# Returning expert results to their tokens: one DRAM row per token and choice in place of selection products

## The reference, cut to what matters

```
logits = h @ router                       # 256 x 8
top_vals, top_idx = top_k(logits, 2)      # two experts for each token
gates = softmax(top_vals)
gate_e = sum(one_hot(top_idx) * gates)    # 256 x 8, zero where not chosen
for e in range(8):
    out = out + gate_e[:, e] * ((silu(h @ wg[e]) * (h @ wu[e])) @ wd[e])   # 1024 -> 3584 -> 1024
x = x + out;  x = rmsnorm(x, final_norm)
```

## Time and profile before

| | us |
|---|---|
| three runs | 2585.18, 2580.52, 2580.43 |
| median | 2580.52 |
| span of the profiled execution | 2584.9 |
| PE busy | 2500.7 (97%) |
| DVE busy | 1807.1 (70%) |
| ACT busy | 1447.6 (56%) |
| POOL busy | 71.3 (3%) |
| DRAM read, written | 633.07 MB, 7.86 MB |

### The profile page before, as it was taken

How to read it: one execution, slowest core, us unless ns; L and a number is a source line. 1 busy time by engine, 2 the same in 40 slices (tenths; PEclk the granted TensorE clock), 3 DMA queues, 4 the chain that set the end, 5 groups by cost and what they waited for, 6 DMA issues and landing times.

```text
span 2584.9 us, 32744 instructions
## 1 busy us (share of the span) xinstructions
PE 2500.7 (97%) x11767; PEld 1991.6 (77%) x11767; DVE 1807.1 (70%) x1708; ACT 1447.6 (56%) x1564; POOL 71.3 (3%) x54
## 2 busy tenths in 40 slices
PE   7999999989999999999999998999999999998999
PEld 6678887667788888888888786888884687777887
DVE  6564446557999999989998986645544575777544
ACT  4554434546777777777777775435443343466443
POOL 0000000011000000000000000600000000000000
PEclk9999999889999999999999999999999999999999
DMA  6885542659999999999999996655543344434652
GB/s 219 313 312 180 192 165 98 245 179 360 393 371 365 367 371 365 363 368 361 365 357 388 341 346 221 227 186 188 184 162 118 119 131 135 131 98 162 228 191 69
DMA packets 330911, 642.13 MB, mean 248 GB/s; under 512 B 14441, under 2 KB 113289, under 8 KB 330633
## 3 DMA queue, kind: packets, MB, share of 16 engines
q1 hardware_dynamic: 328088, 631.02, 69.8%
q0 software_dynamic: 2736, 9.96, 1.0%
HBM read 633.07 MB, written 7.86 MB: 248 GB/s over the span
## 4 chain that ended last, share of the span: by engine, by line
PE 87%; DVE 6%; ACT 4%; DMA 2%; issue 1%; SPq 0%; POOL 0%; DVEq 0%; ACTq 0%; POOLq 0%
PE ps L950 21%; PE ps L863 19%; PE ps L990 11%; PE ps L905 10%; PE ps L1370 6%; PE ps L795 5%; PE ps L1399 2%; PE ps L1301 2%; PE ps L1104 1%; PE ps L838 1%; DVE As L2403 1%; PE ps L876 1%; PE ps L975 1%; DVE Bs L2493 1%; DVE ringL L2373 1%
## 5 line engine op out<-in xcount | busy, mean ns | idle before, releaser
L2403 DVE TENSOR_TENSOR As<-ringA,As 128x2048 fp32r<-128x2048 f32 x316 | 727.0, 2301 | 188.0 <-ACT As L1690 115.6
L950 PE MATMUL ps<-As,xgs 128*128 128x512 f32 x2688 | 646.3, 392 | 7.7 <-DVE As L2403 6.2
L950 PEld LDWEIGHTS ps<-As,xgs 128*128 128x128 f32 x2688 | 498.9, 188 | 114.7 <-issue 5.3
L1779 ACT ACTIVATE As<-ringA 128x2048 fp32r<-128x2048 f32 x224 | 428.8, 1914 | 107.4 <-PE ps L950 101.9
L863 PE MATMUL ps<-As,xs 128*128 128x512 f32 x1408 | 361.3, 394 | 0.0
L990 PE MATMUL ps<-Bs,hds 128*128 128x512 f32 x1320 | 319.4, 391 | 4.1 <-DVE hds L2474 2.5
L863 PEld LDWEIGHTS ps<-As,xs 128*128 128x128 f32 x1408 | 261.9, 188 | 55.9
L990 PEld LDWEIGHTS ps<-Bs,hds 128*128 128x128 f32 x1320 | 246.4, 188 | 60.2 <-issue 7.3
L2493 DVE TENSOR_TENSOR Bs<-ringB,Bs 128x2048 fp32r<-128x2048 f32 x110 | 251.8, 2289 | 19.6 <-ACT Bs L1818 18.6
L905 PE MATMUL ps<-Bs,hds 128*128 128x512 f32 x1056 | 247.9, 390 | 0.0
L1818 ACT ACTIVATE Bs<-ringB 128x2048 fp32r<-128x2048 f32 x110 | 211.2, 1920 | 63.4 <-PE ps L990 62.1
(11 more groups left out here) (424 smaller groups left out, 3228.5 us busy)
## 6 DMA issues: line engine op xcount, KB each, us to landing
ringA<-in_moe_w_gate SPq DMA_DIRECT2D x112, 1024.0 KB, 6.9
ringA<-in_moe_w_up SPq DMA_DIRECT2D x112, 1024.0 KB, 6.7
ringB<-in_moe_w_down SPq DMA_DIRECT2D x112, 1024.0 KB, 6.9
ringA<-in_w_ff_in SPq DMA_DIRECT2D x132, 512.0 KB, 4.7
ringA<-in_w_in SPq DMA_DIRECT2D x56, 1024.0 KB, 5.3
ringA<-in_w_ada SPq DMA_DIRECT2D x36, 1024.0 KB, 6.5
ringB<-in_w_ff_out SPq DMA_DIRECT2D x33, 1024.0 KB, 5.0
ringA<-in_dense_w_gate SPq DMA_DIRECT2D x28, 512.0 KB, 3.6
```

What stands on the lines that cost most here:

```text
L950: m = mm(ps[:, bank, :], lhs(l, tt, k), As[:, h, r, k % 4, :], start=k == 0 and n == 0, stop=k == KC - 1 and n == 2)
L1779: A(As[:, h, 0, :, :], ringA[:, (p["a"] + u) % 2, 4 * h:4 * h + 4, :], ACT.Copy).then_inc(A_high, 1)
L2403: V.tensor_tensor(As[:, h, 1, :, :], ringA[:, (p["a"] + u) % 2, 4 * h:4 * h + 4, :], f32(As[:, h, 0, :, :]), ALU.subtract).then_inc(A_spli ...
```

## The change

- The results of an expert are no longer brought back by products. `one_hot` (gated), the transposes of `selg`, `gate_sums`, `y_low`, `scatter`, `add` and the idle products go.
- A DRAM tensor `results` has a row per token and choice (512), and rows beyond for slots without a token. It is cleared by POOL with four more DMAs behind the nine of `taken`.
- A DRAM tensor `owner` holds for each expert and slot the number of the result row and the gate. POOL fills it first with rows beyond, then, behind the four writes into `taken`, writes it with four indirect DMAs of eight bytes per token and choice, waits for them, and loads it into `slot_of`. `places()` works out `mine` (row number and gate) before it lets POOL go on (`placed` 6 instead of 4).
- ACT's `keep_y` copies the expert's gate column (1 column), waits for that copy and for the expert before's write to have landed, writes `ye` unrounded in fp32 and itself frees the accumulator. POOL then writes `ye` to `results` with one indirect DMA per expert.
- After the eighth write has landed, POOL loads the two halves of `results`, each 1 MB, into `hT` and the arena; DVE adds both to x (128x2048 each) behind the first block of `ff0c`. The final norm and the transposes that follow it come one block later than before in each stream, and `head` is 3 instead of 2.
- If the second path is taken, `mine` points beyond the 512 rows, and what DVE adds is the cleared zeros.

```diff
+SKIP = 2 * SEQ
+NROWS = 2 * SKIP + P
...
+    parts["row"] = np.arange(P)[:, None] + P * np.arange(2 * TILES)[None, :]
...
+        results = nc.dram_tensor("results", (NROWS, D), F32, kind="Internal").ap()
+        owner = nc.dram_tensor("owner", ((NE + 1) * P, 2), U32, kind="Internal").ap()
+        mine = sb("mine", [P, 2 * TILES, 2], U32)
+        slot_of = sb("slot_of", [P, NE + 1, 2], U32)
...
-        ye = arenaR[:, 1024:1024 + D], hTR[:, 0:4, :].rearrange("p k n -> p (k n)")
+        ye = ar(1024, D)
+        returned = hT[:, :, :].rearrange("p k n -> p (k n)"), ar(0, TILES * D)
...
             def turn_taken(e):
                 pe.wait_ge(rows_back, 16 * e)
-                if not isinstance(e, int) or e >= 2:
-                    pe.wait_ge(added, 2 * e - 2)
+                pe.wait_ge(xg_ready, 2 * e)
...
-            def scatter(e, tt):
...
-                    for q in range(2):
-                        last = mm(ps[:, bank + half, :], selT[:, tt, :], ye[q][:, half * 512:(half + 1) * 512], start=q == 0, stop=q == 1)
-                last.then_inc(mixed_back, 1)
...
                 def after(n):
-                    if n in (2, 3) and not first:
-                        scatter(e - 1, n - 2)
-                    if n == NB1 - 2:
-                        pe.wait_ge(selg_ready, e + 1)
-                        for tt in range(TILES):
-                            last = tr(ps[:, 3, tt * P:(tt + 1) * P], selg[:, tt, :], ident)
-                        last.then_inc(selg_tp, 1)
-                        if not final:
-                            turn_taken(e + 1)
+                    if n == NB1 - 2 and not final:
+                        turn_taken(e + 1)
...
                 expert(NE - 1)
-                idle_products(2)
-                for tt in range(TILES):
-                    scatter(NE - 1, tt)
...
# GpSimd
+            for g in range(2 * TILES):
+                pool.dma_start(results[g * P:(g + 1) * P, :].rearrange("p (a b) -> p a b", a=4), blank.unsqueeze(1).broadcast_to([P, 4, 256])).then_inc(cleared, 16)
...
+            pool.dma_start(owner.rearrange("(e s) c -> s e c", s=P), slot_of[:, :, :]).then_inc(unnamed, 16)
...
-            pool.wait_ge(placed, 4)
+            pool.wait_ge(placed, 6)
             for j in range(2 * TILES):
                 pool.indirect_dma_start(out=taken[:, :], ...).then_inc(put, 16)
+            pool.wait_ge(unnamed, 16)
+            for j in range(2 * TILES):
+                pool.indirect_dma_start(out=owner[:, :], out_offset=bass.IndirectOffsetOnAxis(ap=place[:, j:j + 1], axis=0), in_=mine[:, j, :], in_offset=None).then_inc(named, 16)
+            pool.wait_ge(named, 16 * 2 * TILES)
+            pool.dma_start(slot_of[:, :, :], owner.rearrange("(e s) c -> s e c", s=P)).then_inc(scattered, 16)
+            pool.wait_ge(scattered, 16)
+            for e in range(NE):
+                pool.wait_ge(acc_free, ph["moe"]["f"] + e + 1)
+                pool.indirect_dma_start(out=results[:, :], out_offset=bass.IndirectOffsetOnAxis(ap=slot_of[:, e, 0:1], axis=0), in_=ye, in_offset=None).then_inc(scattered, 16)
+            pool.wait_ge(scattered, 16 * (NE + 1))
+            for choice in range(2):
+                pool.dma_start(returned[choice].rearrange("p (t n) -> p t n", t=TILES), results[choice * SEQ:(choice + 1) * SEQ, :].rearrange("(t p) n -> p t n", p=P)).then_inc(results_in[choice], 16)
...
# ScalarE
             def keep_y(e):
+                act.wait_ge(scattered, 16 * e + 16)
+                A(small[:, 354:355], slot_of[:, bass.ds(e, 1), 1].bitcast(F32), ACT.Copy).then_inc(gcol_kept, 1)
+                act.wait_ge(gcol_kept, e + 1)
                 act.wait_ge(down_done, e * (2 * NB1) + (ph["moe"]["s"] + 2 * NB1))
-                act.wait_ge(selgT_ready, e + 1)
-                A(ye[0], ps[:, 4:6, :].rearrange("p a b -> p (a b)"), ACT.Copy, scale=small[:, 354:355]).then_inc(y_high, 1)
+                A(ye, ps[:, 4:6, :].rearrange("p a b -> p (a b)"), ACT.Copy, scale=small[:, 354:355]).then_inc(acc_free, 1)
...
# VectorE
             def places():
...
                 V.tensor_copy(place[:, :], to).then_inc(placed, 1)
+                V.tensor_copy(mine[:, :, 1].bitcast(F32), small[:, 310:314])
+                V.tensor_scalar(small[:, 452:453], small[:, 344:345], float(CAP), float(SKIP), ALU.is_gt, ALU.mult).then_inc(placed, 1)
+                dve.wait_ge(placed, 5)
+                V.tensor_scalar(mine[:, :, 0], k1("row"), small[:, 452:453], None, ALU.add).then_inc(placed, 1)
...
             def x_rows(n):
                 if n == 0:
+                    for choice in range(2):
+                        dve.wait_ge(results_in[choice], 16)
+                        last = V.tensor_tensor(flat_x, flat_x, returned[choice], ALU.add)
+                        if choice == 0:
+                            ch.done(last)
+                    last.then_inc(x_ready, 1)
+                if n == 1:
                     dve.wait_ge(nrm_std, SQ["final"])
...
-            feed(ph["ff0c"], 2, ahead=True, head=2, drains=False, after=x_rows, within=x_scale)
+            feed(ph["ff0c"], 2, ahead=True, head=3, drains=False, after=x_rows, within=x_scale)
```

More of the change, by code:

```diff
@@ L1025, in turn_taken @@
                     last.then_inc(gathered, 1)
-            def scatter(e, tt):
-                if tt == 0:
-                    pe.wait_ge(acc_free, e + (moe["f"] + 1))
-                    if not isinstance(e, int) or e < NE - 1:
-                        pe.wait_ge(xg_ready, 2 * e + 4)
-                final = isinstance(e, int) and e == NE - 1
-                if final != bool(tt):
-                    pe.wait_ge(added, 2 * e + tt)
-                bank = 2 if final and tt else 6
-                for half in range(2):
-                    for q in range(2):
-                        last = mm(ps[:, bank + half, :], selT[:, tt, :], ye[q][:, half * 512:(half + 1) * 512], start=q == 0, stop=q == 1)
-                last.then_inc(mixed_back, 1)
             def expert(e):
@@ L2070, in x_rows @@
             def x_rows(n):
-                if n == 1:
+                if n == 2:
                     act.wait_ge(x_ready, XR["moe"])
                     squares(lambda tt: x[:, tt, :], 1, 1e-5, lambda tt, q: x_tok[:, tt, :])
-                if n in (2, 3):
-                    tt = n - 2
+                if n in (3, 4):
+                    tt = n - 3
                     scale, shift = mod_cols(0, 0)
@@ L2101, in context_end @@
                     stats(call["mixc"], [(x_ready, XR["ff0c"])], lambda tt: cs[:, tt, :], eps=1e-6)
-            feed(ph["ff0c"], 2, ahead=True, head=2, drains=False, before=x_rows, within=x_stats)
+            feed(ph["ff0c"], 2, ahead=True, head=3, drains=False, before=x_rows, within=x_stats)
             feed(ph["ff0x"], 2, head=2, leads=False, before=context_end)
@@ L2552, in after @@
                         context_low(n)
-                    if n == 2 and not first:
-                        add(e - 1, 0)
                     if n == 3 and first:
                         places()
-                    if n == 4:
-                        if not first:
-                            dve.wait_ge(selg_tp, e)
-                        one_hot(e, e + 2, True)
                     if n == NB1 - 2 and not final:
@@ L2566, in body @@
                     nxt = (i + 1, 0) if u else (i, 1)
-                    if isinstance(i, int) and i == 1 and u == 0 and not first:
-                        y_low(e - 1)
-                    if last:
-                        gate_sums(e)
                     if not u and not lead:
                         pair_low(e, i - 1)
-                    if isinstance(i, int) and i == 2 and u == 0 and not first:
-                        add(e - 1, 1)
                     if last and final:
@@ L2581, in body @@
                         unit_low(e, *nxt, 0)
-                        y_low(e)
                         unit_low(e, *nxt, 1)
@@ L2879, in _ @@
                 expert(NE - 1)
-                for tt in range(TILES):
-                    add(NE - 1, tt)
-                dve.wait_ge(added, TILES * NE)
             with dve.Else():
```

73 lines of the change are left out of this document (27 added, 46 removed).

## The result

The changed kernel takes 2568.83 us (median of 9 runs, 2563.09 to 2574.25) against 2580.52 (median of 9) for the kernel before. The ratio is 0.9947, 95% interval 0.9933 to 0.996, so 10 to 17 us less. The forecast was 2562.3 us with a range of 2554 to 2576. The profiled execution took 2574.08 us with a span of 2572.3, so it lies 5.3 us above its median, about as the profiled execution of before (2585.2) lies above its own.

The account below looks back on a forecast made before the run. PE was taken to set the pace of the expert loop. The terms, -17.1 - 6.1 + 1.5 + 2.5 + 1.0 = -18.2 us from the 2580.5 us median, gave 2562.3 us, range 2554 to 2576.

Parts of the forecast that it names:

- term 4: Early clearing of result rows: four more clears delay the dense_w_up load near 150 us, +2.5 us, bounds 0 and 5.4.
- Term 1: Expert loop: PE's products, transposes and waits for the hidden block's split go, -17.1 us, at least 12.9.
- Term 2: After the last expert: shorter road to the next feed and less half-speed clock, -6.1 us, bounds 4.6 and 6.4.
- Term 3: Return of the rows after the last write: PE stalls in the feed's second block, +1.5 us, bounds 0 and 9.
- term 5: Places and owners in expert 0: more small DVE operations and small-element transfers, +1.0 us, bounds 0.5 and 3.
- A: Rival: late return of the rows costs 9 instead of 1.5 us, 2569.8 us; chance 0.17.
- B: Rival: early clears and small elements at their upper ends, 5.4 and 3 us, 2567.2 us; chance 0.12.
- C: Rival: DVE becomes the bound in the expert loop and eats the whole 17.1 us, 2579.4 us; chance 0.05.
- D: Rival: the DMA queue bounds the expert loop at 366 GB/s, slower than before, 2589.9 us; chance 0.06.

Follow-up runs that it names:

- c1: Changed kernel plus two idle 128x512 identity products in each of experts 1 to 7, no added DVE work: 2582.4 us, ratio 1.0007 to the kernel before.
- c4: Kernel before without the products of the low part of the expert's result (4 of 8 per expert): 2576.45 us, ratio 0.9982.
- d1: Changed kernel with a2's wait, a later wait for two places, one more weight pair before expert 0's rows, idle products before the last down group: 2553.83 us.
- a1: Changed kernel with only the first fill of the owners moved behind three blocks of the dense feed: 2566.06 us, ratio 0.9926 to the kernel before.
- e3: Changed kernel with the four new clears and the owners' fill moved late, the nine old clears early: 2558.89 us, ratio 0.9912 to the kernel before.
- b1: Kernel before plus only the four clears of the result rows behind the nine old ones: ratio 1.0031, 8.0 us more.
- b2: Kernel before with its nine old clears moved behind the third block of the dense part: ratio 0.9994.
- a2: Changed kernel with all thirteen clears and the owners' fill moved behind three blocks of the dense feed: 2555.49 us, ratio 0.989 to the kernel before.
- c2: Changed kernel with each expert's rows written five times, four of them to tensors nobody reads: 2582.5 us, ratio 1.0001 to the kernel before.
- e2: Changed kernel with only the four new clears moved behind the third dense block, the owners' fill staying early: 2565.8 us, ratio 0.9942 to the kernel before.

## Why the prediction was right, term by term

The range of 2554 to 2576 us holds 2568.8, and the direction and the main mechanism were right: PE's work removed in the loop comes off the end. That the time is as near as 6.5 us to the forecast of 2562.3 is in part luck: term 4 was 7.4 us too low, and the other terms together 7.9 us too high.

| term | predicted | read from the profile after |
|---|---|---|
| 1 loop | -17.1 | -20.7 |
| 2 after the last expert | -6.1 | -7.4 |
| 3 return of the rows | +1.5 | 0 |
| 4 clears, and the fill that was left out of it | +2.5 | +9.9 |
| 5 places and owners in expert 0 | +1.0 | -0.5 |
| sum | -18.2 | -18.7 |

**Term 1** had the right mechanism and was 3.6 us too small. Products and transposes were sized rightly (c1, c4). The time that came with them was about 0.9 us per expert and not 0.35. I had counted only the wait that the list names, and that list counts from the modelled end of the product before, 0.39 us after its start, while products follow each other every 0.23. From start to start the named place has 0.74 us where 0.23 is usual, and 0.33 behind it: 0.6 us. The rest lies in smaller gaps of PE's row of products; which engine made each of them isn't shown. Six periods give 17.8 us, and the last expert, up to its last down group, 2.9.

**Term 2** had 4.6 us for the shorter road and 1.5 for the clock. The road gave 4.15. The reason for the clock was wrong: the half-speed stretch did not go, it moved from the feed to the last down group, where the feed does not feel it: d1 had that group at full speed and its feed began no earlier. What gained 3.25 us by the feed's fifth block was that its first block ran at full speed and that the 1.4 us wait of its third block vanished.

**Term 3** came out at 0, the lower bound. The step that failed is the landing of the last write. I took the 9.8 to 10.9 us of four writes in a row; the last one alone was there within 4.7 us of its issue (1554.84 to 1559.53). That it was alone is not enough, for the seven in the loop were alone too and took 8.9 us in the median, with the engines at share 1.03; from 1554 to 1560 the share was 0.55. The two returns then took 10.3 and 13.0 us, as I had thought. The fit in the Trainium skill, "DMA: Bandwidth & Descriptors", section Anatomy of one DMA, has 3.2 us for the write and 6.8 for the loads: nearer than mine for the first, too low for the second, and right in that the stall is 0.

**Term 4** is the large miss. Its failing step is that the clears "bite only after" 148.5 us and then share the engines half and half, by which only 2.6 of their 5.4 us would reach the weights. In fact the old clears already had the engines to themselves when the load was issued (102.0% from 144 to 146), and with the new ones behind them the weights got 19.2% until 158. So about all of the added bytes came first: 4.9 us (a1 against e3) to 6.3 us (b1), near or over the upper bound. And one part of the change was missing altogether: term 5 counted the 1152 small pieces where the owners are read back, in expert 0, but nobody counted the fill that writes as many of them at 145 us, 3.9 us. Both meet at the place where the chain hangs on one load, and PE had no idle time behind it.

**Term 5** can't be judged by the one pair. Over all profiles without an edit in this stage, expert 0 takes 113.2 us in the mean of the eight with the change and 111.5 in the mean of the four without it, 1.7 us more, where 1.0 was forecast and -0.5 stands in the table. Both groups spread by 2 to 3 us.

**The rest.** The terms sum to -18.7 us, but the medians fell by 11.7, and the ratio gives 10 to 17. For the two profiled executions the gap can be closed. Outside the terms they differ by +4.3 us ahead of the stretch, -2.9 between the dense part and expert 0, and +4.6 behind the feed's fifth block, so with the table's -18.7 it is -12.7, and the span shrank by 12.6. The first of these is chance: it lies before anything of the change has run, and there, from 78 to 88 us, the changed kernel's profile has its clock at 0.50 and the kernel before 1.00. In the thirteen profiles the stretch begins anywhere from 132.9 to 139.6 us, with the change or without. Between whole times, the mean granted clock is part of it: 0.9861 over the changed kernel's runs, against 0.9889 for 23 of the kernel before. 0.0028 of 2570 us is at most 7 us (an estimate, as if PE set the time throughout), or 14 us more at half speed. It goes with the early transfers: the six kernels that have neither the four clears nor the fill early (b2, a2, e3, c4, d1 and the kernel before) have means of 0.9878 to 0.9895, the seven that have one or both 0.9845 to 0.9870. At most 10.2 of the 14 us lie in one half-speed stretch that I can name, behind PE's stall at 163 to 174 us. Why the remainder falls into the same kernels isn't shown; single profiles differ by more than that in where such stretches lie.

**The rivals.** A (late return) did not happen here, but is a real mechanism (c2: 10.95 us of stall). B (the early clears and small elements at their upper ends) did happen at the first place, worse than priced, together with a larger gain. Its 2567.2 us and A's 2569.8 both lie within 2 us of the result, so the time alone would have pointed to a late return that did not happen. C (DVE as the bound) is refuted: PE busy 121.00 of 121, DVE 107.89. D (DMA as the bound of the loop) is refuted: it decided at 370 GB/s, and the loop ran at 380 (45.1 MB in 118.7 us) and, in c2, at 397. The Trainium skill's 358 and 368 GB/s for one core (same page, section Specifications) are not the limit that this kernel meets.

## What to carry to other kernels

Before a transfer is put "early, where it costs nothing", look at how full the DMA engines are there, and by which queue. At share 1.00 the four clears (2.1 MB, 5.2 us at 404 GB/s) delayed the load that the chain waits for by about their full time, and a fill in 8-byte pieces cost many times its bytes (3.9 us at 404 GB/s would be 1.6 MB, and it is 9 KB). Move such preparation to a stretch where the engines have room; here one wait gave back as much as the whole change had brought. When a resource looks like a ceiling (share 1.00, 366 GB/s), ask whether anyone waits for it, since here it was only the demand. And when a forecast comes true, check its terms one by one: this one held while its fourth term was four times too small.

## What the runs showed of the hardware that was not expected

- 1152 pieces of 8 bytes (9 KB) held the 16 DMA engines for some 4 us, at 123 and 187 GB/s and a share of 1.25 and 0.99, where 404 were moved before (102 and 174 GB/s in e2); 128 pieces of 72 bytes did not (337 and 363).
- While the software queue sent its clears, it had 84.5% of the engines' time and the weights on the hardware queue 19.2% (150 to 158 us of the changed kernel), with 741 and 546 packets, 2.68 and 0.54 MB.
- One core's DMA moved 397 GB/s through the five periods of 119.0 us in c2 with PE busy throughout, at the price of landings of 11.1 us for 1 MB (7.0 to 7.5 at 382).
- An indirect write of 0.5 MB (128 rows) landed in 8.9 us in the median inside the loop and in 4.4 behind it; the four clears, issued behind nine others on the software queue, took up to 23.6.
- Behind a stall of 11 us in PE, caused by DMA, the clock was granted at half speed for 10.2 us (163.4 to 173.6 in the changed kernel).
